# Expert weights in one array, larger transfers from the ninth pair on, and the last two blocks one by one

## What is computed

```python
def hier_moe(xn, w_rg, b_rg, w_re, b_re, w_gate, w_up, w_down):
    ...
    for e in range(N_EXPERTS):
        h = jax.nn.silu(xt @ w_gate[e]) * (xt @ w_up[e])
        y = y + combine[:, e:e + 1] * (h @ w_down[e])
```

## Time and profile before

| | us |
|---|---|
| median of 3 runs | 1200.93 (1200.26 to 1201.15) |
| the profiled execution | 1200.14 |
| its span, first to last instruction | 1198.3 |
| PE busy in it | 1126.8 (94%) |

### The profile page before, as it was taken

The page is one execution under the profiler, slowest core; times in us unless marked ns, Lnnn a source line. Parts: engine busy times, 40 slices in busy tenths (PEclk is TensorE's granted clock), DMA queues, the critical chain, the costliest instruction groups (busy, mean ns, idle before and its releaser), DMA issues.

```text
span 1198.3 us, 13942 instructions
## 1 busy us (share of the span) xinstructions
PE 1126.8 (94%) x4998; PEld 504.3 (42%) x4998; DVE 221.0 (18%) x581; ACT 233.7 (20%) x546; POOL 115.6 (10%) x307
## 2 busy tenths in 40 slices
PE   8999989999999988889999999899999998888897
PEld 6776543333333332223387755333333332222232
DVE  2765350000000000000223234400000000000002
ACT  2144131111121111111112232311121111111111
POOL 0002111100011000000000000200001000000001
PEclk9999999999999999999999999999999999999999
DMA  6984589999999999999998364899999999999994
GB/s 237 336 349 180 215 311 398 427 421 428 428 428 428 429 429 429 428 426 428 423 368 330 106 229 173 313 418 429 418 429 427 429 428 428 428 428 428 428 428 190
DMA packets 49450, 444.33 MB, mean 371 GB/s; under 512 B 9660, under 2 KB 14840, under 8 KB 17656
## 3 DMA queue, kind: packets, MB, share of 16 engines
q1 hardware_dynamic: 48040, 441.34, 88.8%
q10 hardware_dynamic: 1360, 2.31, 0.6%
HBM read 442.54 MB, written 1.09 MB: 370 GB/s over the span
## 4 chain that ended last, share of the span: by engine, by line
PE 65%; DMA 29%; DVE 4%; issue 1%; ACT 1%; SPq 0%; POOL 0%; POOLq 0%; ACTq 0%; DVEq 0%
PE PS L1534 23%; PE PS L1543 12%; DMA places<-in_moe_w_up 12%; DMA places<-in_moe_w_gate 11%; PE PS L1284 8%; PE PS L1550 6%; DMA places<-in_moe_w_down 6%; PE PS L1416 5%; PE PS L1288 4%; PE PS L1296 1%; PE PS L1371 1%; PE PS L1503 1%; PE PS L1400 1%; PE PS L1601 1%; PE PS L1585 1%
## 5 line engine op out<-in xcount | busy, mean ns | idle before, releaser
L1534 PE MATMUL PS<-places,mix 128*64 128x512 f32 x1984 | 442.1, 595 | 43.4 <-DMA places<-in_moe_w_up 29.5
L1534 PEld LDWEIGHTS PS<-places,mix 128*64 128x64 f32 x1984 | 142.3, 137 | 335.1 <-issue 281.2
L1543 PE MATMUL PS<-places,gain_att 128*64 128x512 f32 x960 | 215.1, 599 | 4.0 <-ACT gain_att L809 3.5
L1550 PE MATMUL PS<-mix 128*128 128x512 f32 x256 | 124.8, 608 | 0.0
L1543 PEld LDWEIGHTS PS<-places,gain_att 128*64 128x64 f32 x960 | 66.4, 137 | 129.8 <-issue 124.9
L762 ACT ACTIVATE mix<-acts 128x512 f32 x120 | 76.3, 636 | 226.6 <-PE PS L1534 214.3
L1284 PE MATMUL PS<-acts,places 128*128 128x256 f32 x448 | 103.2, 384 | 0.0
L1185 DVE TENSOR_TENSOR mix<-PS,mix 128x512 f32<-128x512 f32 x30 | 20.7, 692 | 426.2 <-PE PS L1534 418.0
L1284 PEld LDWEIGHTS PS<-acts,places 128*128 128x128 f32 x448 | 83.2, 190 | 14.9 <-issue 3.1
L527 POOL TENSOR_TENSOR sm<-sm 128x1 f32<-128x1 f32 x32 | 6.2, 193 | 697.6 <-PE PS L1608 697.5
L566 POOL TENSOR_SCALAR mix<-drop 128x64 f32<-128x64 f32 x128 | 72.0, 579 | 0.0
(11 more groups left out here) (218 smaller groups left out, 626.1 us busy)
## 6 DMA issues: line engine op xcount, KB each, us to landing
places<-in_moe_w_gate SPq DMA_DIRECT2D x56, 2048.0 KB, 25.1
places<-in_moe_w_down SPq DMA_DIRECT2D x54, 2048.0 KB, 32.5
places<-in_moe_w_up SPq DMA_DIRECT2D x52, 2048.0 KB, 30.3
places<-in_moe_w_gate SPq DMA_DIRECT2D x16, 1024.0 KB, 10.2
places<-in_moe_w_up SPq DMA_DIRECT2D x16, 1024.0 KB, 6.2
places<-in_moe_w_down SPq DMA_DIRECT2D x16, 1024.0 KB, 8.1
places<-in_c_w_in SPq DMA_DIRECT2D x12, 1024.0 KB, 20.5
places<-in_ab_w_in SPq DMA_DIRECT2D x8, 1024.0 KB, 13.8
```

The source lines that it names most:

```text
L1534: last = mm(PS[e * SLOTS:(e + 1) * SLOTS, 2 + part, :], xg[:, k, e * SLOTS:(e + 1) * SLOTS], w[e][:, kk, :], start=(k == 0), stop=(k == NK ...
L1543: last = mm(PS[e * SLOTS:(e + 1) * SLOTS, 6 + b, :], hidT[:, k, e * SLOTS:(e + 1) * SLOTS], w[e][:, 512 * b:512 * b + 512], start=(k == 0) ...
L1550: last = mm(PS[:, Y_BANK[q]], pickT[:, t], ye[:, 512 * b:512 * b + 512], start=first, stop=final)
```

## The change

One array, `moe_w_experts`, takes the place of the three: for each layer and pair it is 128 partitions x 12 chunks, so that one partition's 12 chunks (96 KB) lie together. A row of a transfer is still in one piece, but the next partition's row is 96 KB on.

`group_of` says which chunks travel together: one by one in pairs 0 and 1, two by two in pairs 2 to 7, and from the ninth pair (i = 8) on chunks 0-1, 2-5, 6-9 and 10-11, that is 2, 4, 4 and 2 MB. The last pair of a layer (`end`) goes two by two, and its chunks 10 and 11 one by one, each with its own signal. SP waits for all the places of a group before it issues the transfer.

In `last_pair` chunk 10 becomes an ordinary `down_chunk`, and chunk 11 a block of its own; the signal `s_left` still follows the first output half of chunk 11.

On both SP and PE the loop covers pairs 8 to 11 only, in one round; pairs 4 to 7 are written out on PE, and pairs 12 to 15 on both.

```diff
+def group_of(i, c, end=False):
+
+    if i < 2 or end and c >= CHUNKS - 2:
+        return c, 1
+    if i >= 2 * ROUND and not end:
+        return (0, 2) if c < 2 else (2, 4) if c < 6 else (6, 4) if c < 10 else (10, 2)
+    return c - c % 2, 2
...
-            def two_chunks(l, pair, i, c):
-
-                src, j = block_of(c)
+            def some_chunks(l, pair, i, c, n):
+
                 p = place_of(i, c)
-                dst = places[:, p:p + 2, :].rearrange("p c n -> p (c n)")
-                sp.dma_start(dst, src[l, bass.ds(pair, 1), j // 2].rearrange("o p c n -> p (o c n)")).then_inc(s_place[l][p], 16)
+                dst = places[:, p:p + n, :].rearrange("p c n -> p (c n)")
+                sp.dma_start(dst, w_experts[l, bass.ds(pair, 1), :, c:c + n].rearrange("o p c n -> p (o c n)")).then_inc(s_place[l][p], 16)
...
-                with sp.Fori(0, trips // ROUND - 2) as g:
+                rounds = sp.snap(sp.value_load(more_passes[0:1, 0:1], min_val=0, max_val=MAX_PASSES - 1) * (PAIRS // ROUND)
+                                 + (PAIRS // ROUND - 3))
+                with sp.Fori(0, rounds) as g:
                     for i in range(2 * ROUND, 3 * ROUND):
-                        for c in range(0, CHUNKS, 2):
-                            sp.wait_ge(s_used[l], g * (ROUND * CHUNKS) + used_before(i, c + 1))
-                            two_chunks(l, (g * ROUND + i) % PAIRS, i, c)
+                        for c, n in groups(i):
+                            sp.wait_ge(s_used[l], g * (ROUND * CHUNKS) + used_before(i, c + n - 1))
+                            some_chunks(l, (g * ROUND + i) % PAIRS, i, c, n)
+                for i in range(2 * ROUND, 3 * ROUND):
+                    for c, n in groups(i, i == 3 * ROUND - 1):
+                        sp.wait_ge(s_used[l], rounds * (ROUND * CHUNKS) + used_before(i, c + n - 1))
+                        some_chunks(l, PAIRS - 3 * ROUND + i, i, c, n)
...
                     pe.wait_ge(s_hT[l], i + 2)
+                    down_chunk(n, rounds, 2, True)
+                    chunk_there(n, CHUNKS - 1, rounds, True)
                     for b in range(2):
-                        for k in range(NF // 2, NF):
-                            if b == 0:
-                                chunk_there(n, 2 * UP_CHUNKS + k, rounds)
-                            for e in range(AT_ONCE):
-                                last = mm(PS[e * SLOTS:(e + 1) * SLOTS, 6 + b, :], hidT[:, k, e * SLOTS:(e + 1) * SLOTS],
-                                          slot(n, 2 * UP_CHUNKS + k, e)[:, 512 * b:512 * b + 512], start=False, stop=(k == NF - 1))
+                        for e in range(AT_ONCE):
+                            last = mm(PS[e * SLOTS:(e + 1) * SLOTS, 6 + b, :], hidT[:, NF - 1, e * SLOTS:(e + 1) * SLOTS],
+                                      slot(n, CHUNKS - 1, e)[:, 512 * b:512 * b + 512], start=False, stop=True)
                         if b == 0:
                             last.then_inc(s_left, 1)
-                    last.then_inc(s_used[l], NF // 2)
+                    last.then_inc(s_used[l], 1)
```

More of the change, by code:

```diff
@@ L91, in place_of, with groups, signal_of, loads_a_round @@
     return (i * CHUNKS + c - (ONCE if (i, c) >= (KEPT, OUT_CHUNKS) else 0)) % PLACES
[L94 to L102, removed]
+def group_of(i, c, end=False):
[4 more added lines that the diff above has]
+    return c - c % 2, 2
+def groups(i, end=False):
+    out, c = [], 0
+    while c < CHUNKS:
+        n = group_of(i, c, end)[1]
+        if once(i, c) is None:
+            out.append((c, n))
+        c += n
+    return out
+def signal_of(i, c, end=False):
+    return place_of(i, group_of(i, c, end)[0])
+def loads_a_round(i, c, end):
+    p = signal_of(i, c, end)
+    return sum(place_of(n, first) == p for n in range(2 * ROUND, 3 * ROUND) for first, _ in groups(n))
+def loads(layer, i, c, end=False):
+    p = signal_of(i, c, end)
     mixer = p < IN_CHUNKS[layer] or p >= CHUNKS
-    return mixer + sum(once(*n) is None and signal_of(*n) == p and (n[0] < 2 or place_of(*n) == p) for n in
-                       [divmod(m, CHUNKS) for m in range(i * CHUNKS + c + 1)])
+    return mixer + sum(place_of(n, first) == p and (n, first) <= (i, c) for n in range(i + 1) for first, _ in groups(n, end and n == i))
 def left_at(p):
@@ L195, in build @@
 def build(nc, x, x_turned, gain0, t5, ln_mix, ln_ffn, ln_final, ab_in, ab_out, lam, subln, c_in, c_out, rel,
-          w_rg, b_rg, w_re, b_re, w_gate, w_up, w_down, consts, hot_t5, hot_rel, out):
+          w_rg, b_rg, w_re, b_re, w_experts, consts, hot_t5, hot_rel, out):
     ctx = ExitStack()
@@ L442, in chunk @@
                     for e in range(AT_ONCE):
-                        sp.dma_start(slot(i, c, e), src[l, pair, j // 2, :, j % 2, e * w:(e + 1) * w]).then_inc(signal, 16)
+                        sp.dma_start(slot(i, c, e), w_experts[l, pair, :, c, e * w:(e + 1) * w]).then_inc(signal, 16)
                     return
-                sp.dma_start(whole(i, c), src[l, bass.ds(pair, 1), j // 2, :, j % 2].rearrange("o p n -> p (o n)")).then_inc(signal, 16)
-            def two_chunks(l, pair, i, c):
-                src, j = block_of(c)
+                sp.dma_start(whole(i, c), w_experts[l, pair, :, c]).then_inc(signal, 16)
+            def some_chunks(l, pair, i, c, n):
                 p = place_of(i, c)
-                dst = places[:, p:p + 2, :].rearrange("p c n -> p (c n)")
-                sp.dma_start(dst, src[l, bass.ds(pair, 1), j // 2].rearrange("o p c n -> p (o c n)")).then_inc(s_place[l][p], 16)
+                dst = places[:, p:p + n, :].rearrange("p c n -> p (c n)")
+                sp.dma_start(dst, w_experts[l, bass.ds(pair, 1), :, c:c + n].rearrange("o p c n -> p (o c n)")).then_inc(s_place[l][p], 16)
             for l in range(DEPTH):
@@ L497, in _ @@
                 for i in range(2, 2 * ROUND):
-                    for c in range(0, CHUNKS, 2):
-                        if once(i, c) is None:
-                            sp.wait_ge(s_used[l], used_before(i, c + 1))
-                            two_chunks(l, i, i, c)
+                    for c, n in groups(i):
+                        sp.wait_ge(s_used[l], used_before(i, c + n - 1))
+                        some_chunks(l, i, i, c, n)
                 sp.wait_ge(s_go[l], 1)
                 trips = sp.snap(sp.value_load(more_passes[0:1, 0:1], min_val=0, max_val=MAX_PASSES - 1) * PAIRS + PAIRS)
-                with sp.Fori(0, trips // ROUND - 2) as g:
+                rounds = sp.snap(sp.value_load(more_passes[0:1, 0:1], min_val=0, max_val=MAX_PASSES - 1) * (PAIRS // ROUND)
+                                 + (PAIRS // ROUND - 3))
+                with sp.Fori(0, rounds) as g:
                     for i in range(2 * ROUND, 3 * ROUND):
-                        for c in range(0, CHUNKS, 2):
-                            sp.wait_ge(s_used[l], g * (ROUND * CHUNKS) + used_before(i, c + 1))
-                            two_chunks(l, (g * ROUND + i) % PAIRS, i, c)
+                        for c, n in groups(i):
+                            sp.wait_ge(s_used[l], g * (ROUND * CHUNKS) + used_before(i, c + n - 1))
[4 more added lines that the diff above has]
+                        some_chunks(l, PAIRS - 3 * ROUND + i, i, c, n)
             for q, signal, count in ((0, s_xn, DEPTH * NT + 1), (1, s_xua, NK // 2 + 1), (3, s_xn, DEPTH * NT + 2)):
@@ L1506, in experts, with chunk_there @@
             def experts(l):
-                def chunk_there(n, c, rounds):
+                def chunk_there(n, c, rounds, end=False):
                     if once(n, c) is not None:
@@ L1512, in chunk_there, with up_chunk @@
                     else:
-                        pe.wait_ge(s_place[l][signal_of(n, c)], rounds * (16 * (ROUND * CHUNKS // PLACES)) + 16 * loads(l, n, c))
-                def up_chunk(i, first, n, rounds, c):
+                        pe.wait_ge(s_place[l][signal_of(n, c, end)], rounds * (16 * loads_a_round(n, c, end)) + 16 * loads(l, n, c, end))
+                def up_chunk(i, first, n, rounds, c, end=False):
                     part = c // UP_CHUNKS
@@ L1528, in up_chunk @@
                         pe.wait_ge(s_pkT[l], i)
-                    chunk_there(n, c, rounds)
+                    chunk_there(n, c, rounds, end)
                     w = [slot(n, c, e).rearrange("p (k n) -> p k n", k=KPU) for e in range(AT_ONCE)]
@@ L1536, in up_chunk, with down_chunk @@
                     last.then_inc(s_used[l], 1)
-                def down_chunk(n, rounds, k):
-                    chunk_there(n, 2 * UP_CHUNKS + k, rounds)
+                def down_chunk(n, rounds, k, end=False):
+                    chunk_there(n, 2 * UP_CHUNKS + k, rounds, end)
                     w = [slot(n, 2 * UP_CHUNKS + k, e) for e in range(AT_ONCE)]
@@ L1561, in last_pair @@
                     for c in range(2 * UP_CHUNKS):
-                        up_chunk(i, False, n, rounds, c)
```

(26 more changed lines are left out.)

7 lines of the change are left out of this document (1 added, 6 removed).

## The result

The changed kernel takes 1208.6 us (median of 4 runs, 1207.2 to 1208.8), the kernel before 1200.6 us on the same chip: ratio 1.0067, 95% interval 1.0055 to 1.0080. It is 8.0 us slower; 9.1 us had been forecast. The profiled execution took 1208.4 us.

The account below looks back on a forecast made before the run. PE bounds the kernel until 390 us, then DMA landings until the layer's end. Lag 6.8, clock 1.7 and code 0.6 sum to +9.1 us, forecasting a median of 1210.0 us, range 1202 to 1217.

Parts of the forecast that it names:

- The wait for four chunks: Fifteenth pair: chunks 6 and 7 wait for 8 and 9, so PE ends each layer 3.4 us later, 6.8 in all.
- Nothing absorbs it: Last pair's 27.5 us of work against 29.4 of landing makes good hardly any delay; nothing behind the first layer does either.
- one of its own signs of being wrong: The prediction named PE's work in the last pair turning out shorter than 27.5 us as showing it wrong.
- The clock: PE's longer waits before chunk 6 may lower its granted clock: 0 to 1.7 us a layer, one fall taken, +1.7.
- The split: Last two chunks signalled one by one: 1.8 us a layer if PE waits there, nothing in the changed kernel.
- The rival's 1195.5 us: PE makes up its delay before chunk 10, so each layer gains 1.8 + 0.9 = 2.7 us: 1195.5 us, chance 10%.
- the lag: PE's delay from chunks 6 to 9 of the fifteenth pair sharing a transfer: last pair begins at 568.1 instead of 564.05.
- Larger transfers: 14 transfers of 4 MB a layer, rows of 32 KB: loads end 0.9 us earlier in each layer, bounds 0 to 1.9.
- A fixed cost of about 2 us for each transfer: Rival: joining transfers saves a fixed cost; at 0.5 us each, 1195.5 us again. Chance 2%.
- The rows' spacing: Rows 96 KB apart in expert loads: taken as 0; as a rival, loads 1.4% slower, 1223 us, chance 8%.
- SP's waits: SP waits for four free places, issuing up to 4 us later; enough is queued ahead, so cost nothing.
- Code: Written-out pairs fetch some four more code blocks a layer: 0.3 us a layer, +0.6, bounds 0 to 2.4 a layer.

Follow-up runs that it names:

- e8: The changed kernel, but chunks 6 to 9 of each layer's fifteenth pair come as two transfers of 2 MB: ratio 0.9994 to the kernel before.
- e5: The changed kernel, but the fifteenth pair's chunks 6 to 11 come in one transfer of 6 MB: 1219.1 us, ratio 1.0158 to the kernel before.
- e6: The changed kernel with three useless matmuls before chunk 6 of the fifteenth pair, where PE waits: 1205.2 us, ratio 1.0043 to the kernel before.
- e3: The changed kernel with a layer's last two chunks in one 2 MB transfer and one block, as before: 1208.6 us, ratio 1.0068 to the kernel before.
- e1: The changed kernel with 2 MB transfers instead of 4 MB; array, written-out pairs and split last two chunks stay: ratio 1.0002 to the kernel before.
- e10: The kernel before with the one array alone; its loops, 2 MB transfers and last block stay: 1199.0 us, ratio 0.9993 to the kernel before.
- e4: The kernel before with only the one array and the written-out pairs; 2 MB transfers, last two chunks together: 1201.0 us, ratio 1.0009.

## Why the prediction was right, and where it was off

**The wait for four chunks** was the step that carried it. Chunk 6 of the fifteenth pair was put 4.0 us later (4.9 for one more landing of two chunks, 0.9 gained by DMA); it came 3.7 and 4.8 us later. e8 shows that the loss goes with this transfer, e5 that it grows by a landing when two chunks are added.

**Nothing absorbs it.** The last pair's own work had been put at 27.5 us, by subtracting 0.6 us of waiting from 28.1. Without any wait it took 26.8, by which the forecast was 0.7 us a layer too high; a shorter last pair was one of its own signs of being wrong. The printed waits of 0.6 us were only half of the waiting. The other half are gaps at the restarts that the timeline doesn't print: from the pair's first chunk (564.05 before, 567.71 in the change) to its second it was 4.8 us before and is 4.6 now, with no wait printed in either.

```profile
568.84 3.65 PE L1534 MATMUL PS<-places,mix 128*64 128x512 f32 x16
572.30 3.65 PE L1554 MATMUL PS<-places,mix 128*64 128x512 f32 x16
```

**The clock.** Bounds of 0 to 1.7 us a layer, one fall of two taken; both layers had one, 1.7 us each. The mechanism and the size of one fall were right; the count was a guess and missed, 3.4 us where 1.7 had been put. e6 shows the mechanism by removing it. Why the wait of 2.5 us at 433 had none isn't settled.

**The split** was rightly put at nothing in the changed kernel (e3). The step that failed is its price in the rivals: "half of the block, 1.8 us, would leave the path in each layer, if PE were waiting there". PE was waiting there, but for a printed 0.33 us only. From chunk 9 to the scatter it took 5.85 us before and 5.30 in e1, so the gain is 0.55 us; all the waiting of the last pair together is 1.3. The rival's 1195.5 us, 2.7 a layer, was therefore out of reach; the kernels with the split and without the lag came in at ratios of 0.9987 to 1.0002, some 1199 to 1201 us.

**Larger transfers**: 0.9 us a layer earlier. From the first expert matmul, chunks 8 and 9 landed at 393.2 (388.3 + 4.9) and 394.9 us before, and at 392.0 and 394.9 after: 1.2 and 0.1. The last load landed at 427.4 and 429.1 us before, and at 426.6 and 429.0 after: 0.9 and 0.1. The term is right in one layer and nothing in the other. A fixed cost of about 2 us for each transfer, as the Trainium skill has it (SBUF — State Buffer, "The DMA setup-cost knee"), isn't to be seen: by an estimate from it the joined transfers would have brought 28 us a layer.

**The rows' spacing** cost nothing (e10: 428 GB/s, ratio 0.9993). The Trainium skill (DMA: Bandwidth & Descriptors, "Latency and other measured facts") reports lower rates at row pitches of 512 KB and larger powers of two; at 96 KB no such loss appeared.

**SP's waits** were put at nothing. In the change the DMA share is 1.00 and the rate 430 GB/s between 340 and 560 us, so the DMA engines didn't run dry.

**Code**: four blocks a layer as estimated, priced at 0.6 us in all; e4 and e10 leave between nothing and some 3 us.

Together, for the two layers:

| us | forecast | in the trace |
|---|---|---|
| chunk 6 of the fifteenth pair later, code included | 8.0 + 0.6 | 3.7 + 4.8 = 8.5 |
| the clock | 1.7 | 1.7 + 1.7 = 3.4 |
| the last pair shorter | -1.2 | -1.3 - 1.2 = -2.5 |
| sum | 9.1 | 9.4 |

That the sums agree so well is in part luck: the second fall of the clock (+1.7) was left out, and the last pair's work was put too high (-1.3 in the two layers). The measured 8.3 of the spans and 8.0 of the medians are smaller still because of what lies outside the two stretches, -1.1 us, which no run explains. For the same reason the sign "the last chunk's block ends 3 to 6 us later than 592.2" fails as it was written: it ended at 594.6, 2.4 later, and 4.1 only when both are counted from the first expert matmul.

## What to carry to other kernels

A transfer is usable when all of it has landed, so joining two moves the first half's landing back by the second half's time; that is free while the consumer can catch up, and is paid in full for the last transfers before work that has no slack. Before making transfers larger, find the last place where the consumer still waits and compare its own work from there on with the landing time that is left. A finer or earlier transfer gives back at most the time in which the consumer is idle at that place, not the length of the block behind it. That idle time is best taken from the distance between two starts, compared with the same stretch where nothing waits, because the printed waits here were only half of it.

## What the runs showed of the hardware

A stretch with two thirds of its bytes in 4 MB transfers, in rows of 32 KB that start 96 KB apart, moved at about the rate of one with 2 MB transfers alone: 430 GB/s between 340 and 560 us of the change, 428 before. And a wait of some 2.6 us in a stretch where PE is otherwise busy was followed, in nine of thirteen cases, by a block at a lower granted clock (0.57 and 0.65 in the two windows above) that took up to 1.7 us longer; useless matmuls in the wait before the fifteenth pair's chunk 6 brought that back in both layers.

```profile
340.00:560.00 220.00, 199.44 (x837) 68.61 (x834) 13.35 (x22) 33.01 (x55) 20.77 (x56) 0.97 1.00 430
```
